# A three-layer transformer kernel: attention weights scaled on GpSimd before they are transposed, eight biases moved there, and the top-k search cut into four parts

## What is computed

```python
s = q @ k.T * 64 ** -0.5 + bias        # group A: -slope*dist + log(multiplicity)
                                       # group B: -slope*dist, -inf where not in the top 128
p = exp(s - max(s)); o = (p / p.sum(-1)) @ v
x = x + gate * (concat(o) @ w_out)
_, idx = top_k(where(causal, indexer_score, -inf), 128)
```

## Time and profile before

| | |
|---|---|
| median of three runs | 1987.98 us |
| the profiled execution, its own time | 1991.48 us |
| its span in the trace | 1989.7 us |
| TensorE busy | 1923.1 us, 97% of the span |
| VectorE, ScalarE, GpSimd busy | 1034.7, 451.9, 1184.4 us |
| granted TensorE clock over the span | 0.985 of full speed |

### The profile page before, as it was taken

The page is one execution under the profiler, slowest core; times in us unless marked ns, Lnnn a source line. Parts: engine busy times, 40 slices in busy tenths (PEclk is TensorE's granted clock), DMA queues, the critical chain, the costliest instruction groups (busy, mean ns, idle before and its releaser), DMA issues.

```text
span 1989.7 us, 25330 instructions
## 1 busy us (share of the span) xinstructions
PE 1923.1 (97%) x8824; PEld 1551.2 (78%) x8824; DVE 1034.7 (52%) x1529; ACT 451.9 (23%) x774; POOL 1184.4 (60%) x907
## 2 busy tenths in 40 slices
PE   5999999999999999999999999999988899999998
PEld 4787868888888887667788888887766688888886
DVE  7566256666655453466766663233877453323222
ACT  3302342211210022352221211112228421111100
POOL 3743326788887955324688787746540256666773
PEclk7999999999999999999999999999989999999999
DMA  7432223455554422111455553322210023222332
GB/s 305 177 117 75 96 95 106 170 190 192 204 193 174 172 96 85 53 52 55 157 191 193 197 189 117 105 96 85 74 59 17 27 82 104 95 95 95 106 105 74
DMA packets 67375, 242.23 MB, mean 122 GB/s; under 512 B 7498, under 2 KB 7882, under 8 KB 67314
## 3 DMA queue, kind: packets, MB, share of 16 engines
q1 hardware_dynamic: 65536, 237.01, 34.2%
q10 hardware_dynamic: 1778, 4.37, 0.6%
HBM read 239.25 MB, written 2.10 MB: 121 GB/s over the span
## 4 chain that ended last, share of the span: by engine, by line
PE 86%; DVE 7%; ACT 3%; issue 2%; DMA 2%; POOL 1%; DVEq 0%; SPq 0%; ACTq 0%; POOLq 0%
PE gemm L447 23%; PE gemm L448 23%; PE gemm L449 23%; DMA w_raw<-wstream 2%; DVE b_score L1630 1%; PE mix L650 1%; PE gemm L474 1%; PE gemm L476 1%; PE gemm L475 1%; DVE b_top L1625 1%; PE mix L447 1%; PE gemm L1046 1%; PE gemm L803 1%; DVE sq_acc L1365 1%; PE mix L449 1%
## 5 line engine op out<-in xcount | busy, mean ns | idle before, releaser
L431 POOL TENSOR_TENSOR w_lo<-w_raw,w_hi 128x1024 fp32r<-128x1024 f32 x302 | 734.9, 2433 | 25.2
L447 PE MATMUL gemm<-h_hi,w_hi 128*128 128x512 f32 x1616 | 634.0, 392 | 20.8 <-DVE h_lo L1186 14.6
L448 PE MATMUL gemm<-h_lo,w_hi 128*128 128x512 f32 x1616 | 630.1, 390 | 0.0
L449 PE MATMUL gemm<-h_hi,w_lo 128*128 128x512 f32 x1616 | 630.1, 390 | 0.0
L428 POOL TENSOR_TENSOR pool_gate<-pool_gate 128x1 f32<-128x1 f32 x298 | 118.3, 397 | 734.4 <-PE gemm L449 592.8
L447 PEld LDWEIGHTS gemm<-h_hi,w_hi 128*128 128x128 f32 x1616 | 304.2, 188 | 90.2 <-issue 21.8
L429 POOL TENSOR_SCALAR w_hi<-w_raw 128x1024 fp32r<-128x1024 f32 x302 | 344.1, 1139 | 17.5 <-DMA w_raw<-wstream 17.5
L449 PEld LDWEIGHTS gemm<-h_hi,w_lo 128*128 128x128 f32 x1616 | 304.0, 188 | 63.8
L448 PEld LDWEIGHTS gemm<-h_lo,w_hi 128*128 128x128 f32 x1616 | 304.1, 188 | 62.0
L1080 DVE CUSTOM_DVE_ANT_0 ada_raw<-ada_raw,c_act 128x1024 f32<-128x1024 f32 x128 | 216.5, 1707 | 110.1 <-DMA ada_raw<-adastream 110.1
L449 PE MATMUL gemm<-p_hi,w_lo 128*128 128x512 f32 x528 | 205.4, 389 | 0.0
(11 more groups left out here) (339 smaller groups left out, 1972.0 us busy)
## 6 DMA issues: line engine op xcount, KB each, us to landing
w_raw<-wstream SPq DMA_DIRECT2D x302, 512.0 KB, 3.5
ada_raw<-adastream SPq DMA_DIRECT2D x128, 512.0 KB, 4.3
a_early<-adastream SPq DMA_DIRECT2D x8, 1024.0 KB, 11.9
out<-x_res SPq DMA_DIRECT2D x8, 256.0 KB, 2.2
c_act<-c_in ACTq DMA_DIRECT2D x2, 512.0 KB, 7.2
x_res<-x_in SPq DMA_DIRECT2D x2, 512.0 KB, 6.3
x_res<-x_in ACTq DMA_DIRECT2D x2, 512.0 KB, 9.0
b_dist<-const_in ACTq DMA_DIRECT2D x1, 512.0 KB
```

The source lines that it names most:

```text
L431: pool.tensor_tensor(wlo[s][:], raw[:, u % RAW, :], whi[s][:].bitcast(F32), ALU.subtract).then_inc(w_split, 1)
L447: pe.matmul(out_ap, w_h, r_h, start=first, stop=False)
L448: pe.matmul(out_ap, w_h, r_l, start=False, stop=False)
L449: return pe.matmul(out_ap, w_l, r_h, start=False, stop=last)
```

## The change

GpSimd multiplies each head's exponentials in `Z` by the reciprocal row sums (`unit_rows`, four instructions per head, each with a per-partition scalar from `rsm`) and releases the transposes by `att_n`. `inverse_rows`, the copy to `rows` and `normalised` are gone: `values` now gives the final result, `pair_high` and `pair_low` read it from PSUM, and `values(p)` waits for `pair_low(p-1)`. The pieces of a pair are five where they were six with the rows, so their numbers in the semaphores change and the banks alternate over pairs. The eight biases of group A are made on GpSimd in two instructions each (`pool_bias`): four behind the split of chunk 223, the others at the head of the loop over pairs. GpSimd's loop over chunks is cut around the stage; chunks 224 to 227 are split ahead of `unit_rows(0)`, 228 and 229 behind it.

The search runs as 4, 8, 2 and 2 rounds: `logits(0)` and `logits(1)` come behind the first twelve rounds, `inverse_sums(0)`, `logits(2)` and `logits(3)` behind fourteen, the mask behind sixteen. The biases of group B stay on VectorE, in rounds p = 2 to 5, both behind `pair_low(p-1)`. On ScalarE `pair_high(p-1)` goes ahead of copies 2 and 3, and bank 3 is the first of the value banks copied; `scores(0)` waits for it only at its fourth matmul.

```diff
 EARLY_ROUNDS = 4
+MID_ROUNDS = 8
...
 @block.gpsimd
+            def pool_bias(g):
+                if g >= 4:
+                    pool.wait_ge(sig("att_z"), g - 3)
+                if g < 8:
+                    pool.tensor_scalar(BI[:, g % 4, 0:T], DL[:, 0:T], -SLOPE_A[g], None, ALU.mult).then_inc(sig("att_bs"), 1)
+                    pool.wait_ge(sig("att_bs"), g + 1)
+                    pool.tensor_tensor(BI[:, g % 4, 0:T], BI[:, g % 4, 0:T], DL[:, T:2 * T], ALU.add).then_inc(sig("att_b"), 1)
+            def unit_rows(p):
+                pool.wait_ge(sig("att_r"), p + 1)
+                for a in range(2):
+                    z = Z[(2 * p + a) % 4]
+                    for j in range(NTB):
+                        q = 8 * (p % 2) + 4 * a + j
+                        o = slice(OFF_J[j], OFF_J[j] + P * (j + 1))
+                        ins = pool.tensor_scalar(z[:, o], z[:, o], rsm[:, q:q + 1], None, ALU.mult)
+                    ins.then_inc(sig("att_n"), 1)
+            early = N0["attn_in"] + 14
+            late = N0["attn_out"] + 4
+            groups(1, early // 4)
+            chunks(early // 4 * 4, early)
+            pool.wait_ge(small_loaded, 96)
+            for g in range(4):
+                pool_bias(g)
+            chunks(early, late - 2)
+            unit_rows(0)
+            chunks(late - 2, late)
+            for p in range(8):
+                if p < 2:
+                    pool_bias(2 * p + 4)
+                    pool_bias(2 * p + 5)
+                if p + 1 < 8:
+                    unit_rows(p + 1)
+            chunks(late, -(-late // 4) * 4)
...
 @block.tensor
             def scores(p):
                 if p == 0:
                     pe.wait_ge(sig("vb_copied"), 4)
-                    pe.wait_ge(gfree[3], G0["attn_out"][3])
...
+                    if p == 0 and b == 4:
+                        pe.wait_ge(gfree[3], G0["attn_out"][3])
...
             def turn(p, pieces):
                 for c in pieces:
-                    pe.wait_ge(sig("att_e"), 2 * p + (1 if c < 2 else 2))
-                    slot(p, c)
+                    pe.wait_ge(sig("att_n"), 2 * p + (1 if c < 2 else 2))
+                    slot(5 * p + c)
...
-            def inverse_rows(p):
-                pe.wait_ge(sig("att_r"), p + 1)
-                slot(p, 5)
-                for j in range(NTB):
-                    for a in range(2):
...
             def values(p):
...
-                    pe.wait_ge(sig("att_y"), p)
-                pe.wait_ge(sig("att_c"), 6 * p + 5)
+                    pe.wait_ge(h_ready, KT * 7 + p)
+                pe.wait_ge(sig("att_c"), 5 * p + 5)
...
 @block.vector
-            largest(TOPK // 8 - EARLY_ROUNDS)
+            largest(MID_ROUNDS)
...
             def logits(g):
...
-                dve.wait_ge(sig("att_b"), g + 1)
+                if g < 8:
+                    dve.wait_ge(sig("att_b"), g + 1)
                 if g >= 4:
-                    dve.wait_ge(sig("att_t"), 6 * (g // 2 - 2) + 5)
+                    dve.wait_ge(sig("att_t"), 5 * (g // 2 - 2) + 5)
...
             def inverse_sums(p):
                 dve.wait_ge(sig("att_e"), 2 * p + 2)
+                if p >= 2:
+                    dve.wait_ge(sig("att_n"), 2 * p - 2)
...
-            def normalised(p):
-                dve.wait_ge(sig("att_o0"), p + 1)
-                dve.wait_ge(sig("att_o1"), p + 1)
-                dve.wait_ge(sig("att_c"), 6 * p + 6)
-                dve.tensor_tensor(sqt[:, p % 2, :], G[2][:], rows[:], ALU.mult).then_inc(sig("att_y"), 1)
...
             def pair_low(k):
                 dve.wait_ge(hhi_ready, KT * 7 + k + 1)
-                dve.tensor_tensor(Hlo[:, k, :], sqt[:, k % 2, :], Hhi[:, k, :].bitcast(F32), ALU.subtract).then_inc(h_ready, 1)
+                dve.tensor_tensor(Hlo[:, k, :], G[2][:], Hhi[:, k, :].bitcast(F32), ALU.subtract).then_inc(h_ready, 1)
...
-            for g in range(4):
-                bias(g)
-            for g in range(4):
-                logits(g)
+            logits(0)
+            logits(1)
+            rest = TOPK // 8 - EARLY_ROUNDS - MID_ROUNDS
+            largest(rest // 2)
             inverse_sums(0)
+            logits(2)
+            logits(3)
+            largest(rest - rest // 2)
+            excluded()
             for p in range(8):
-                if p + 2 < 8:
-                    bias(2 * p + 4)
-                if p >= 1:
-                    normalised(p - 1)
-                if p + 2 < 8:
-                    bias(2 * p + 5)
                 if p >= 1:
                     pair_low(p - 1)
+                if 2 <= p < 6:
+                    bias(2 * p + 4)
+                    bias(2 * p + 5)
                 if p + 1 < 8:
                     inverse_sums(p + 1)
...
 @block.scalar
-            for j in range(4):
+            for j in (3, 0, 1, 2):
                 act.activation(VA[:, j, :], G[j][:], ACT.Copy).then_inc(gfree[j], 1)
...
             def pair_high(k):
-                act.wait_ge(sig("att_y"), k + 1)
-                act.activation(Hhi[:, k, :], sqt[:, k % 2, :], ACT.Copy).then_inc(hhi_ready, 1)
+                act.wait_ge(sig("att_o0"), k + 1)
+                act.wait_ge(sig("att_o1"), k + 1)
+                act.activation(Hhi[:, k, :], G[2][:], ACT.Copy).then_inc(hhi_ready, 1)
...
                 if p + 1 < 8:
                     exps(2 * p + 3)
-                copy_turned(p, (2, 3))
                 if p >= 1:
                     pair_high(p - 1)
-                copy_turned(p, (4, 5))
+                copy_turned(p, (2, 3, 4))
```

More of the change, by code:

```diff
@@ L436, in _, with groups, chunks @@
                 split_at(u, 0, u, u >= SPL)
[L437 to L441, removed]
+            def groups(first, last):
+                with pool.Fori(first, last) as b:
+                    for u in range(4):
+                        split_at(4 * b + u, b, u, True)
+            def chunks(first, last):
+                for n in range(first, last):
+                    split_at(n, n // 4, n % 4, True)
+            def pool_bias(g):
[31 more added lines that the diff above has]
+            chunks(late, -(-late // 4) * 4)
+            groups(-(-late // 4), NCHUNK // 4)
+            chunks(NCHUNK // 4 * 4, NCHUNK)
         @block.tensor
@@ L1002, in scores, with slot @@
                         mm.then_inc(sig(f"att_s{a}"), 1)
-            def slot(p, c):
-                n = 6 * p + c
+            def slot(n):
                 if n < 2:
@@ L1019, in turn @@
                         for j in range(i, NTB):
-                            mm = pe.transpose(G[c % 2][:, o + P * (j - i):o + P * (j - i) + P],
+                            mm = pe.transpose(G[(5 * p + c) % 2][:, o + P * (j - i):o + P * (j - i) + P],
                                               z[:, OFF_J[j] + i * P:OFF_J[j] + (i + 1) * P], const("ident"))
                     mm.then_inc(sig("att_t"), 1)
-            def inverse_rows(p):
-                pe.wait_ge(sig("att_r"), p + 1)
-                slot(p, 5)
-                for j in range(NTB):
-                    for a in range(2):
[L1030 to L1034, removed]
             def values(p):
@@ L1061, in _ @@
                 turn(p, (2, 3, 4))
-                inverse_rows(p)
                 values(p)
-            pe.wait_ge(sig("att_c"), 48)
+            pe.wait_ge(sig("att_c"), 40)
             tiles("attn_out", 2)
@@ L1637, in _, with excluded @@
             dve.tensor_scalar(T2[:, 5, :], T2[:, 5, :], col("kv_g"), None, ALU.mult).then_inc(sig("ckv_n"), 1)
-            largest(TOPK // 8 - EARLY_ROUNDS)
[L1640 to L1643, removed]
-            def bias(g):
[L1647 to L1654, removed]
+            largest(MID_ROUNDS)
+            def excluded():
+                dve.tensor_scalar(SC[:, seg(0)], SC[:, seg(0)], 0.5 * NEG, NEG, ALU.is_lt, ALU.mult)
+                for j in range(1, NTB):
+                    ins = dve.tensor_scalar(SC[:, seg(j)], SC[:, seg(j)], 0.5 * TAKEN, NEG, ALU.is_gt, ALU.mult)
+                link(ins)
+            def bias(g):
+                for j in range(NTB):
+                    ins = dve.scalar_tensor_tensor(out=BI[:, g % 4, seg(j)], in0=DL[:, 384 - P * j:T], scalar=-SLOPE_B[g - 8],
+                                                   in1=SC[:, seg(j)], op0=ALU.mult, op1=ALU.add)
+                link(ins)
             def logits(g):
@@ L1706, in _ @@
                     logits(2 * p + 5)
-            normalised(7)
             pair_low(7)
@@ L2111, in copy_turned @@
                 for c in pieces:
-                    act.wait_ge(sig("att_t"), 6 * p + c + 1)
+                    act.wait_ge(sig("att_t"), 5 * p + c + 1)
+                    bank = G[(5 * p + c) % 2]
                     if c < 4:
-                        dst = PS[:, c // 2, 512 * (c % 2):512 * (c % 2) + 512]
-                        ins = act.activation(dst, G[c % 2][:], ACT.Copy)
-                    elif c == 4:
```

(14 more changed lines are left out.)

## The result

The changed kernel takes 2009.1 us, the median of four runs (2007.5 to 2011.1), against 1989.6 us for the kernel before, the median of its three runs and a fourth: a ratio of 1.0098, with a 95% interval of 1.0086 to 1.0110. It is slower by 19.5 us. The prediction said no change that can be measured, 1986.9 us, in a range of 1982.5 to 1993.0. Two single executions that took 3250 us (the kernel before) and 4957 us (one of the experiments) are left out of all that follows.

A forecast was written before the change was run, and what follows sets the result against it. A circle through ScalarE and VectorE, 9.58 us a round, was taken to bind the loop. Gains of 13.0 and 0.23 less losses of 9.9, 1.8 and 0.5 left 1.1 us faster, 1986.9 us; range 1982.5 to 1993.0.

The forecast's parts named there:

- The head of the stage: Start of the attention stage: without the waits for banks and logits, first transpose at 1478.3 against 1491.30, gain 13.0 us.
- GpSimd's price: GpSimd's scaling and biases: 2.0 us per head (1.41 to 3.9), 2.1 us per bias of group A.
- The Trainium skill: Guide speaking against GpSimd elementwise work: a head near 3.3 us, the time some 2 us above the median.
- The loop without VectorE's biases: Loop over pairs: old circle shortens to 8.63 us, buffer `Z` binds at 9.35, 0.23 less than before.
- The long rounds: Rounds p = 2 to 5: both biases behind `pair_low` join the circle, 12.05 us, 2.47 more each, 9.9 in all.
- Contention: VectorE's negation of the maxima meets GpSimd's fourth `unit_rows` instruction: 0.3 us for each of six heads, 1.8 us lost.
- Rival B: Loop over pairs: GpSimd is on the path; at 3.9 us per head some 7 us, 1994 us; chance 0.19.
- Rival C: TensorE's clock falls after stands of about 2 us in long rounds: 1.6 us, 1988.5 us; chance 0.11.
- the tail: From exps(14) to `attn_out`: 18.7 us against 18.20, 0.5 lost.
- The range: Whole kernel, 1982.5 to 1993.0 us: from no contention with cheaper tail and shorter rounds to 3.7 us per head.
- Rival A: Loop over pairs: VectorE's biases stay hidden, all eight rounds near 9.35, 10.8 us faster, 1976.1 us; chance 0.10.

The follow-up runs named there:

- with the second operation: The changed kernel with `add 0.0` behind both GpSimd multiplies (scaling of heads and biases): 1991.3 us, ratio 1.0012 to the kernel before.
- the kernel with both edits: The changed kernel with `add 0.0` in both GpSimd multiplies and VectorE's biases ahead of `pair_low`: 1980.4 us, ratio 0.9957 to the kernel before.

## Why the prediction was wrong

| | predicted | after | with the second operation | three of four multiplies left out |
|---|---|---|---|---|
| first transpose behind TensorE's readiness | 27.1 | 27.05 | 27.04 | 27.08 |
| first transpose to exps(4) | 9.5 | 14.30 | 9.85 | 9.91 |
| exps(4) to exps(6) | 9.35 | 14.25 | 9.32 | 10.08 |
| exps(6) to exps(14), four rounds | 48.2 and 1.8 | 56.56 | 49.71 | 48.37 |
| exps(14) to the end of the stage | 18.7 | 22.68 | 19.22 | 19.36 |

All in us.

- **The head of the stage** was right: 13.0 us predicted, 13.1 in the changed kernel, and 13.0 to 13.1 where it is made alone.
- **GpSimd's price** is the step that failed: "I take 2.0, near the first, because there is one tensor input". It measured 4.28. Both ends were too low, "at most 3.9" included. The choice went by the number of inputs; what decides is whether the instruction has a second operation, and the row chosen as the nearest had one. In the stage the heads and dearer biases cost 4.8 us up to exps(4), 4.9 in the next round, 6.6 in the four long ones and 4.0 behind them, the last two in part by the clock. The bias too measured 2.9, not 2.1. The kernel with the second operation ran 0.2% above the forecast and inside the range, so this one term is nearly all of the error.
- **The Trainium skill**, "GPSIMD Engine Reference", "Performance versus the Vector engine", was set aside in the prediction because the row stood at half of its figure. Its 2.6 cycles an element are 2.2 ns (an estimate from the page), and the page gives them for `tensor_tensor`, with two tensor inputs; the prediction put them on a multiply with one. For two inputs the trace agrees: 2.21 us for 1024 elements, 2.2 ns each. The multiply with a single operation took 3.1 ns an element (1.57 us for 512), four of them 3.3, and with the second operation 2.1 us a head are 1.6 ns. So that the figure came nearer than the row was luck: neither was for this form.
- **The loop without VectorE's biases** was right: 9.35 predicted, 9.32 with the second operation, and 9.35 to 9.36 where only `pair_high` was moved.
- **The long rounds** were right: "The circle is 9.58 - 0.95 + 3.42 = 12.05 us". The run nearly without multiplies has 12.09, and ahead of `pair_low` the same biases cost nothing (9.37).
- **Contention** was right in kind and size, 0.33 us a round for 0.3, with cheap multiplies. Where VectorE's biases met the dear ones, both grew, the biases from 3.42 to 4.13 us and a head from 4.27 to 6.06, which was not foreseen.
- **Rival B** is what happened, at 0.19. At 4.28 and 2.9 us two heads and two biases are 14.3 us, and so is the first round. In the long rounds its 3.4 us of slack left 0.88 (4.28 less 3.4), and the turns at a low clock take 0.55 more (1.64 for 1.09): 12.05 + 0.88 + 0.55 = 13.48, against 13.63 measured in three of them. The fourth has 2.1 us more, handed on from GpSimd's biases of the round before. Its price, 7 us, used 3.9 us a head and neither the dearer bias, the clock nor that delay.
- **Rival C**, the clock, was put at 1.6 us and a chance of 0.11. It came in addition: the slow turns of the long rounds (0.55 each), and the tail, at 0.77 of full clock.
- **The range** has a slip at its lower end: the gains that it names, 1.8 and 1.5 us, lead from 1986.9 to 1983.6, not to 1982.5, and are less than the 4 us that its chance of 0.10 speaks of.
- **Rival A** needed the biases hidden, which they are not in the order of the change. Moved ahead of `pair_low`, with the second operation, they are, and that kernel is 9 us faster than before.

Why did a gain of 13 us disappear even at the cheap price? It was not hidden, and contention took little of it: it was given back by the order on VectorE, 12.43 for 9.59 us in each of four rounds, 11.4 us (0.33 of each being contention).

## What to carry to other kernels

A price for an instruction is taken from a row with the same operations, not only the same engine, shape and number of inputs; where no such row exists, the upper end has to be wide, and a probe of a few instructions in idle time settles it. Of a change that brings a gain and a new cost, run the gain alone: here it was worth 0.4 to 0.6% by itself. And in a queue that runs in order, work that nobody waits for stands ahead of the instruction that waits for another engine, not behind it: moving two biases by one place was worth about 3 us a round, once the multiplies were cheap.

## What the runs showed of the hardware

On GpSimd a multiply by a scalar with a single operation took 2.77 us for 1024 elements of 128 partitions, and the same multiply with an added `add 0.0` 1.05 us, 2.6 times less; with a scalar per partition it was 2.85 and 3.21 against 1.61 and 1.12. The form with a single operation was also dearer than `tensor_tensor` with a broadcast operand (2.21 us), so the extra operation is not merely free, it goes with something faster. What that is stays open. GpSimd and VectorE slow each other: beside each other eight biases took 4.13 us for 3.42 and four multiplies 6.06 for 4.27. Single groups of matmuls fell into a low clock: sixteen of `values` took 4.06 us instead of 2.37 in one round of the kernel with both edits, behind stands as short as in its neighbours, and 3.78 and 4.05 in one round of two kernels whose other rounds are 12 us. Whether shorter rounds bring this about is not shown; the tail ran at 0.83 of full clock in the kernel with rounds of 9.35 us where that with 9.59 had 0.91.
